# One kernel for two transformer blocks: rows remade in the first down projection, an absolute value in the bounded gates

## The chip, the cores and the metric

The kernel runs on one core of a Trainium2 chip. The core has TensorE (PE in the profile; PEld is its weight loads), VectorE (DVE), ScalarE (ACT), GpSimd (POOL) and SyncE (SP), which issues the DMAs. The metric is the device time of one execution in microseconds. TensorE's clock is granted at one of two levels, 2.4 GHz (1.00 in the profile) or 1.2 GHz (0.50).

## The reference

Everything is float32. A first block of two layers works on 256 latent tokens and 256 context tokens of width 1024; a second block of two layers works on the 256 latent tokens. The parts that the change touches:

```python
def _modulate(x, g, shift, scale):
    return _rmsnorm(x, g) * (1 + scale) + shift

def _swiglu(h, w1, w3, w2):                      # D_FF = 2816
    return (jax.nn.silu(h @ w1) * (h @ w3)) @ w2

def _forget(f_raw, lb):
    log_f = jnp.logaddexp(jnp.log(lb), jnp.log1p(-lb) + jax.nn.log_sigmoid(f_raw))
    k = (1.0 - lb) * jax.nn.sigmoid(-f_raw)
    return k, log_f

for l in range(DEPTH):                           # first block, DEPTH = 2
    lat = lat + 0.5 * ml[2] * _swiglu(_modulate(lat, norm_ffn1_g[l], ml[0], ml[1]), *ffn1)
    cx = cx + 0.5 * mc[2] * _swiglu(_modulate(cx, norm_ffn1_g[l], mc[0], mc[1]), *ffn1)
    # token mixer: gMLP and a bidirectional gated scan, whose gates come from _forget
    lat = lat + ml[5] * out_lat
    lat = lat + 0.5 * ml[8] * _swiglu(_modulate(lat, norm_ffn2_g[l], ml[6], ml[7]), *ffn2)
    if not last:
        cx = cx + mc[5] * out_cx
        cx = cx + 0.5 * mc[8] * _swiglu(_modulate(cx, norm_ffn2_g[l], mc[6], mc[7]), *ffn2)
```

The bounds `lb` are zero in layer 0, so only layer 1 has the logaddexp. It is computed as max(a, b) + ln(1 + exp(-|a - b|)).

## The kernel before

**Layout.** Tokens lie along the free dimension, channels on the 128 partitions: X is [128, 8 blocks, 512 tokens]. All weights stream from HBM in 272 slots of 1 MB, each 1024 x 256, in the order of the program. Every product is made in three matmuls (L583 to L585, helper `three`): each operand is split into a high part and the rest (WH and WL of the weights, HH and HL or GH and GL of the activations), and high times high, high times rest and rest times high are summed in PSUM. A slot with 256 tokens has 48 such matmuls, with kin = 6 it has 36.

**A slot's way.** SyncE loads RAW once the slot two before has been split. ScalarE copies it to WH in two halves (L1412) when TensorE has finished the slot two before (`mm_done`). VectorE subtracts for the first half of WL (L2016, one operation over 1024 elements), GpSimd for the second half (L1993, four operations over 256). TensorE waits for the first half at a slot's start and for the second at its fifth block (`slot_half`). Two pairs of PSUM banks alternate; a slot can start when the slot two before has been read out (`bank_read`).

**The plan.** `plan_slots` writes out the phases. A feed-forward part has three thirds of 8, 6 and 8 blocks; each third is an `ffn_up` phase (its slots hold w1 and w3 by turns) and a `down` phase of 4 slots. Each engine has its own program over this plan and runs it in order; in most phases it is a hardware loop of two slots (`repeat`), whose first instruction takes the waits ahead of it. After every slot each engine calls `after_slot`, which does its part of the split for the slot two later.

**Norms.** In four places a norm is made by stream (`norm_by_stream`): TensorE goes on with the context's tokens while the norm of the latents is still to come. The slots behind it begin in `pair_by_stream` (L803 on): blocks of 6 matmuls for stream 1, first of slot 0, from block 5 on by turns with slot 1, then `part_sums(3, 0)`, the last column sums of stream 0 (L665, a product of squares with ones), then five more blocks, and then stream 0, block by block behind `h_ready`. The sums go to VectorE's mean (L2150), ScalarE's root, VectorE's reciprocal (L2156) and then to T2 rows (L2162), HH (ScalarE L1468) and HL (L2168).

**The late norm.** The last feed-forward part of the first block (layer 1, 256 tokens) doesn't wait for its norm. Its rows are X times gain, without the norm's factor and without the shift; two more columns hold the shift, so that its matmuls have 258 columns. Behind each slot VectorE multiplies by RSTD (L2275, L2282) and adds the product of the shift (`shifted_up`, copies at L2273 and L2280, SHIFTED, L2287); ScalarE makes Silu (L1544) and GH (L1549), and VectorE then GL (L2033). All three thirds work so. In `down` VectorE adds bank times gate to X (L2444) behind each slot.

**The bounded gates.** In `w_in` of layer 1 the gates of two directions (d = 0, 1) are made behind slots 1 to 7 (`prepare`), in LF[d], KK[d] and T8, each [128, 2048]: VectorE adds a bound (L2749), takes a minimum (L2750), a maximum (L2754) and a difference (L2755); ScalarE makes Exp and Ln of T8 (L1867, L1868); VectorE adds it to LF (L2762). For d = 1 L2749 and L2750 are behind slot 5, L2754 and L2755 behind slot 6, the rest behind slot 7.

Of the kernel before, what the change touches and what calls it, by code (L numbers as in the profile page):

```python
# [28 lines left out]
KB = D // P  # L29
# [30 lines left out]
def plan_slots():  # L60
# [14 lines left out]
    def ffn(l, which, rate, tokens):  # L75
        if l + which == 2:
            plan.append(dict(kind="late_norm", gain="g_ffn2", layer=l, final=False, mods=(6, 7), ada=ada))
        else:
            do_norm(gain=("g_ffn1", "g_ffn2")[which], layer=l, mods=(0 + 6 * which, 1 + 6 * which), tokens=tokens,
                    first=(l == 0 and which == 0))  # L80
        for t, nb in enumerate(THIRDS):
# [4 lines left out]
            phase("ffn_up", nb, nb, rate, tokens=tokens, blocks=nb, layer=l, third=t, shifted=(l + which == 2))  # L86
# [6 lines left out]
            phase("down", 4, 4, rate, tokens=tokens, kin=nb, gate=2 + 6 * which, layer=l, per=1, first=(t == 0))  # L93
# [127 lines left out]
def build(nc, T):  # L221
    ctx = ExitStack()
    with ctx:
# [354 lines left out]
        def _(pe):  # L578
# [159 lines left out]
            def weights_phase(ph, normed, before):  # L738
                kind, N = ph["kind"], ph["tokens"] + (2 if ph.get("shifted") else 0)
                hbase = n.at(h_ready)  # L740
                loop = kind not in ("w_in", "in_even", "in_odd")

# [60 lines left out]
                def pair_by_stream():  # L803
# [21 lines left out]
                    for kb in range(KB):  # L825
                        if kb == ahead:
                            pe.wait_ge(bank_read[1], ph["unit"] + BANK_CREDIT)
                        if kb >= ahead:
                            block(1, 1, kb - ahead)
                        block(0, 1, kb)  # L830
                    part_sums(3, 0)
# [569 lines left out]
        def _(act):  # L1401
# [246 lines left out]
            def down(ph):  # L1648
# [3 lines left out]
                def body(it):  # L1652
                    for s in range(2 * ph["per"]):
                        after_slot(ph, it, s, 2 * ph["per"])
                        if ph["squares"] and s % ph["per"] == ph["per"] - 1:
# [11 lines left out]
                repeat(act, 2, body, ph is not PLAN[-1])  # L1667
# [182 lines left out]
            def prepare(ph, i):  # L1850
# [14 lines left out]
                if i in (3, 7) and l == 1:  # L1865
                    n.take(dve_to_act)
                    link(act.activation(T8[:], T8[:], ACT.Exp))  # L1867
# [138 lines left out]
        def _(dve):  # L2006
# [416 lines left out]

            def down(ph):
# [4 lines left out]
                def body(it):  # L2429
                    for v in range(2):  # L2430
                        for s in range(per):
                            after_slot(ph, it, per * v + s, 2 * per)
                        if v and ph["ends_by_stream"]:
                            add_unit(True, slice(0, N))
                        dve.wait_ge(mm_done, it * (2 * per) + (ph["slot"] + per * v + per))
# [12 lines left out]
                repeat(dve, 2, body, ph is not PLAN[-1])  # L2448
# [287 lines left out]
            def prepare(ph, i):  # L2736
# [8 lines left out]
                if i in (2, 5) and l == 1:  # L2745
# [4 lines left out]
                    link(dve.tensor_tensor(T8[:], lf, bc(LBT[:, 0, d, :], 4), ALU.min))  # L2750
                if i in (2, 6) and l == 1:
                    d = (2, 6).index(i)
                    lf = LF[d][:]
                    link(dve.tensor_tensor(lf, lf, bc(LBT[:, 0, d, :], 4), ALU.max))  # L2754
                    dve.tensor_tensor(T8[:], T8[:], lf, ALU.subtract).then_inc(dve_to_act, 1)  # L2755
# [296 lines left out]
```

## Time and profile before

| | |
|---|---|
| median of 3 runs | 2616.95 us (2616.52 to 2617.7) |
| profiled execution | 2619.17 us, its span 2617.4 us |
| granted clock of TensorE, mean | 0.995 |
| PE busy | 2569.0 us, 98% |
| DVE, ACT, POOL busy | 1222.5, 1105.2, 889.7 us (47%, 42%, 34%) |
| DMA | 376.90 MB, mean 144 GB/s |
| POOL WL L1993 | 889.5 us in 1088 operations |

PE's busy time comes from modelled ends of pipelined matmuls, so the distance from one start to the next tells more than it. The span is that of one execution with the profiler; 1.8 us lie around it. Idle time of an engine counts only if TensorE stands behind it.

### The profile page before, as it was taken

Reading aid. Unit: us, or ns where it says so; the run is one execution under the profiler, and the core shown is the slowest. Engines: PE = TensorE matmul, PEld = TensorE weight load, DVE = VectorE, ACT = ScalarE, POOL = GpSimd, SP = SyncE. Lnnn points to the kernel's source line nnn. Section 1 sums busy time; section 2 is a strip of 40 time slices with the busy share of each in tenths; the row PEclk is TensorE's granted clock in tenths of the full one; section 3 lists DMA queues with packets and bytes.
Section 4 is the critical chain, followed back from the end, with each engine's and each line's share of the span. In section 5 each row is a group of like instructions: output and inputs, shape, how many; then the busy total and the mean of one; then the engine's idle time right before and its main releaser. Section 6 shows DMA issues by size and latency. Waiting matters only on the chain.

```text
span 2617.4 us, 43989 instructions
## 1 busy us (share of the span) xinstructions
PE 2569.0 (98%) x17111; PEld 2290.2 (87%) x17111; DVE 1222.5 (47%) x1865; ACT 1105.2 (42%) x1538; POOL 889.7 (34%) x1092
## 2 busy tenths in 40 slices
PE   7999999999999999999999999999999999999999
PEld 5777779988897777797777798899999999999999
DVE  4222325227752232252232257675567566656754
ACT  4322333635444122244122247544674554446533
POOL 1222222320022222222222226315554455553554
PEclk9999999999999999999999999999999999999999
DMA  7443543330034334433444433234544444552454
GB/s 282 141 168 140 165 149 117 139 128 1 33 120 146 145 145 145 145 110 132 145 145 145 145 138 133 110 109 180 184 169 165 137 161 177 182 185 100 164 188 147
DMA packets 58528, 376.90 MB, mean 144 GB/s; under 512 B 6223, under 2 KB 12007, under 8 KB 14216
## 3 DMA queue, kind: packets, MB, share of 16 engines
q1 hardware_dynamic: 56988, 371.53, 39.2%
q10 hardware_dynamic: 1388, 3.16, 0.8%
q8 instruction: 118, 1.93, 0.3%
q14 instruction: 34, 0.28, 0.0%
HBM read 370.46 MB, written 3.16 MB: 143 GB/s over the span
## 4 chain that ended last, share of the span: by engine, by line
issue 58%; POOL 22%; PE 17%; DVE 1%; POOLq 1%; DMA 0%; ACT 0%; SPq 0%; DVEq 0%; ACTq 0%
POOL WL L1993 22%; PE PSA L583 5%; PE PSA L585 5%; PE PSA L584 5%; PE PSA L1342 0%; POOLq L405 0%; PE PSA L1240 0%; PE PSA L1267 0%; DMA X<-in_x 0%; DMA RAW<-in_weights 0%; PE PSA L665 0%; POOLq L1991 0%; ACT WH L1412 0%; PE PSA L1258 0%; PE PSA L1228 0%
## 5 line engine op out<-in xcount | busy, mean ns | idle before, releaser
L1993 POOL TENSOR_TENSOR WL<-RAW,WH 128x256 fp32r<-128x256 f32 x1088 | 889.5, 846 | 1715.3 <-ACT WH L1412 1715.3
L1412 ACT ACTIVATE WH<-RAW 128x1024 fp32r<-128x1024 f32 x544 | 545.8, 1050 | 936.6 <-PE PSA L585 918.0
L2016 DVE TENSOR_TENSOR WL<-RAW,WH 128x1024 fp32r<-128x1024 f32 x272 | 339.6, 1249 | 1077.5 <-ACT WH L1412 1077.2
L583 PE MATMUL PSA<-HH,WH 128*128 128x512 f32 (+2 forms) x1664 | 596.3, 358 | 9.4 <-DVE WL L2016 3.4
L584 PE MATMUL PSA<-HL,WH 128*128 128x512 f32 (+2 forms) x1664 | 588.6, 354 | 0.0
L585 PE MATMUL PSA<-HH,WL 128*128 128x512 f32 (+2 forms) x1664 | 588.0, 353 | 0.0
L583 PE MATMUL PSA<-GH,WH 128*128 128x256 f32 (+1 forms) x1664 | 527.0, 317 | 6.8 <-DVE GL L2033 5.7
L584 PE MATMUL PSA<-GL,WH 128*128 128x256 f32 (+1 forms) x1664 | 521.0, 313 | 0.0
L585 PE MATMUL PSA<-GH,WL 128*128 128x256 f32 (+1 forms) x1664 | 520.8, 313 | 0.0
L583 PEld LDWEIGHTS PSA<-HH,WH 128*128 128x128 f32 x1664 | 315.7, 190 | 69.0 <-issue 17.6
L585 PEld LDWEIGHTS PSA<-HH,WL 128*128 128x128 f32 x1664 | 315.8, 190 | 43.2
L584 PEld LDWEIGHTS PSA<-HL,WH 128*128 128x128 f32 x1664 | 315.9, 190 | 41.3
L583 PEld LDWEIGHTS PSA<-GH,WH 128*128 128x128 f32 x1664 | 318.0, 191 | 30.2 <-issue 5.4
L584 PEld LDWEIGHTS PSA<-GL,WH 128*128 128x128 f32 x1664 | 318.0, 191 | 18.6 <-issue 0.5
L585 PEld LDWEIGHTS PSA<-GH,WL 128*128 128x128 f32 x1664 | 317.9, 191 | 18.3
L583 PE MATMUL PSA<-H2H,WH 128*128 128x256 f32 x800 | 230.6, 288 | 0.5 <-DVE S L2346 0.5
L584 PE MATMUL PSA<-H2L,WH 128*128 128x256 f32 x800 | 226.3, 283 | 0.0
L585 PE MATMUL PSA<-H2H,WL 128*128 128x256 f32 x800 | 226.3, 283 | 0.0
L583 PEld LDWEIGHTS PSA<-H2H,WH 128*128 128x128 f32 x800 | 153.4, 192 | 2.3 <-issue 1.7
L584 PEld LDWEIGHTS PSA<-H2L,WH 128*128 128x128 f32 x800 | 153.5, 192 | 1.3 <-issue 1.0
L585 PEld LDWEIGHTS PSA<-H2H,WL 128*128 128x128 f32 x800 | 153.4, 192 | 0.0
L2033 DVE TENSOR_TENSOR GL<-T,GH 128x256 f32 (+3 forms) x168 | 136.0, 844 | 16.0 <-ACT GH L1568 10.6
(336 smaller groups left out, 2966.1 us busy)
## 6 DMA issues: line engine op xcount, KB each, us to landing
RAW<-in_weights SPq DMA_DIRECT2D x272, 1024.0 KB, 4.8
ADA<-in_w_ada SPq DMA_DIRECT2D x65, 1024.0 KB, 4.9
Zada<-in_w_ada SPq DMA_DIRECT2D x7, 1024.0 KB, 14.5
scratch_bias<-BREL ACTq DMA_DIRECT2D x1, 2048.0 KB
SUMS<-in_c_sums SPq DMA_DIRECT2D x1, 1664.0 KB, 8.7
TB<-scratch_bias SPq DMA_DIRECT2D x1, 1536.0 KB, 11.8
X<-in_x SPq DMA_DIRECT2D x1, 1024.0 KB, 6.8
X<-in_ctx SPq DMA_DIRECT2D x1, 1024.0 KB, 9.3
```

Of the source, the lines that this page charges most:

```text
L583: pe.matmul(out, a_hi, b_hi, start=start, stop=False)
L584: pe.matmul(out, a_hi, b_lo, start=False, stop=False)
L585: return pe.matmul(out, a_lo, b_hi, start=False, stop=stop)
L1412: act.activation(WH[:, j, 4 * h:4 * h + 4, :], RAW[:, j, 4 * h:4 * h + 4, :], ACT.Copy)\
L1993: ins = pool.tensor_tensor(WL[:, j, kb, :], RAW[:, j, kb, :], WH[:, j, kb, :].bitcast(F32), ALU.subtract)
L2016: dve.tensor_tensor(WL[:, j, 0:4, :], RAW[:, j, 0:4, :], WH[:, j, 0:4, :].bitcast(F32), ALU.subtract)\
L2033: return dve.tensor_tensor(out, value, hi.bitcast(F32), ALU.subtract)
```

## The change

Three edits. First, in the last feed-forward part of the first block only the first third still has the late norm. In its down projection each of the four slots makes two rows anew, now with RSTD and shift: VectorE T2 = X * scale * RSTD, ScalarE HH = T2 + shift, VectorE HL = T2 + shift - HH, between the split of weights and the addition to X (the rows of X that are read are the ones that are added to right behind it). The second and third third take these rows in 256 columns with the plain `ffn_up`. TensorE takes all eight `h_ready` before the second third's loop. Down's loop is written out on VectorE and ScalarE there. Second, `part_sums(3, 0)` stands in front of the last block of slot 0 instead of behind it. Third, in the bounded gates VectorE's minimum becomes a difference, the later difference goes, and ScalarE has an Abs in front of Exp, which takes a scale of -1.

```diff
--- before.py
+++ after.py
@@ -73,6 +73,7 @@
         plan.append(dict(kind="norm", index=norm, slot=slot, unit=unit, ada=ada, **more))
         norm += 1
     def ffn(l, which, rate, tokens):
+        at = len(plan)
         if l + which == 2:
             plan.append(dict(kind="late_norm", gain="g_ffn2", layer=l, final=False, mods=(6, 7), ada=ada))
         else:
@@ -83,14 +84,16 @@
                 plan.append(dict(kind="decays", part=2 * t - 1))
             if l + which == 0 and t:
                 plan.append(dict(kind=("", "setup_loads", "setup")[t]))
-            phase("ffn_up", nb, nb, rate, tokens=tokens, blocks=nb, layer=l, third=t, shifted=(l + which == 2))
+            phase("ffn_up", nb, nb, rate, tokens=tokens, blocks=nb, layer=l, third=t, shifted=(l + which == 2 and t == 0),
+                  renewed=(l + which == 2 and t == 1))
             if l + which == 0 and t == 2:
                 plan.append(dict(kind="bounds"))
             if t == 0:
                 plan.append(dict(kind="gate", layer=l, mod=2 + 6 * which, half=True, ada=ada))
             if l + which == 2:
                 plan.append(dict(kind="decays", part=2 * t))
-            phase("down", 4, 4, rate, tokens=tokens, kin=nb, gate=2 + 6 * which, layer=l, per=1, first=(t == 0))
+            phase("down", 4, 4, rate, tokens=tokens, kin=nb, gate=2 + 6 * which, layer=l, per=1, first=(t == 0),
+                  renews=plan[at] if l + which == 2 and t == 0 else None)
     for l in range(2):
         both, lat = 512, (512 if l == 0 else 256)
         ffn(l, 0, 1, both)
@@ -739,6 +742,8 @@
                 kind, N = ph["kind"], ph["tokens"] + (2 if ph.get("shifted") else 0)
                 hbase = n.at(h_ready)
                 loop = kind not in ("w_in", "in_even", "in_odd")
+                if ph.get("renewed"):
+                    n.take(h_ready, KB)
 
                 def h_block(kb):
                     pe.wait_ge(h_ready, hbase + kb + 1)
@@ -827,8 +832,9 @@
                             pe.wait_ge(bank_read[1], ph["unit"] + BANK_CREDIT)
                         if kb >= ahead:
                             block(1, 1, kb - ahead)
+                        if kb == KB - 1:
+                            part_sums(3, 0)
                         block(0, 1, kb)
-                    part_sums(3, 0)
                     for kb in range(KB - ahead, KB):
                         block(1, 1, kb)
                     for j in range(2):
@@ -1652,6 +1658,12 @@
                 def body(it):
                     for s in range(2 * ph["per"]):
                         after_slot(ph, it, s, 2 * ph["per"])
+                        if ph.get("renews"):
+                            for m in range(2):
+                                n.take(t_ready)
+                                kb = 4 * it + 2 * s + m
+                                act.activation(HH[:, kb, 0:N], T2[:, m, 0:N], ACT.Identity,
+                                               bias=MODS[:, ph["renews"]["mods"][0], kb, 0:1]).then_inc(hh_ready, 1)
                         if ph["squares"] and s % ph["per"] == ph["per"] - 1:
                             v = s // ph["per"]
                             act.wait_ge(bank_read[v], it * 2 + (ph["unit"] + 2 + BANK_CREDIT))
@@ -1664,7 +1676,7 @@
                                     .then_inc(sq_ready, 1)
                 if ph["ends_by_stream"]:
                     return body(0)
-                repeat(act, 2, body, ph is not PLAN[-1])
+                repeat(act, 2, body, ph is not PLAN[-1] and not ph.get("renews"))
                 if ph["squares"]:
                     n.squares += KB
 
@@ -1864,7 +1876,8 @@
                     act.activation(KK[:, d], KK[:, d], ACT.Exp).then_inc(act_to_dve, 1)
                 if i in (3, 7) and l == 1:
                     n.take(dve_to_act)
-                    link(act.activation(T8[:], T8[:], ACT.Exp))
+                    link(act.activation(T8[:], T8[:], ACT.Abs))
+                    link(act.activation(T8[:], T8[:], ACT.Exp, scale=-1.0))
                     act.activation(T8[:], T8[:], ACT.Ln, bias=1.0).then_inc(act_to_dve, 1)
                 if i == 8:
                     vs = VS[:, 0:4 * (N // P)]
@@ -2421,6 +2434,19 @@
                         after_slot(ph, it, per * v + per - 1, 2 * per)
                 n.skip(h_ready, KB)
 
+            def renewed_rows(late, k0, N):
+
+                shift, scale = late["mods"]
+                for m in range(2):
+                    if k0:
+                        dve.wait_ge(h_ready, n.at(h_ready) + k0 + m - 1)
+                    dve.scalar_tensor_tensor(T2[:, m, 0:N], X[:, k0 + m, 0:N], MODS[:, scale, k0 + m, 0:1], RSTD[:, 0:N],
+                                             ALU.mult, ALU.mult).then_inc(t_ready, 1)
+                for m in range(2):
+                    n.take(hh_ready)
+                    dve.scalar_tensor_tensor(HL[:, k0 + m, 0:N], T2[:, m, 0:N], MODS[:, shift, k0 + m, 0:1],
+                                             HH[:, k0 + m, 0:N].bitcast(F32), ALU.add, ALU.subtract).then_inc(h_ready, 1)
+
             def down(ph):
 
                 if ph["feeds"]:
@@ -2432,6 +2458,8 @@
                             after_slot(ph, it, per * v + s, 2 * per)
                         if v and ph["ends_by_stream"]:
                             add_unit(True, slice(0, N))
+                        if ph.get("renews"):
+                            renewed_rows(ph["renews"], 4 * it + 2 * v, N)
                         dve.wait_ge(mm_done, it * (2 * per) + (ph["slot"] + per * v + per))
                         for m in range(2):
                             for s, t in streams(N):
@@ -2445,7 +2473,9 @@
                             ins.then_inc(bank_read[v], 1)
                 if ph["ends_by_stream"]:
                     return body(0)
-                repeat(dve, 2, body, ph is not PLAN[-1])
+                repeat(dve, 2, body, ph is not PLAN[-1] and not ph.get("renews"))
+                if ph.get("renews"):
+                    n.skip(h_ready, KB)
                 if ph["rate"]:
                     rows_copy(ph)
 
@@ -2747,12 +2777,11 @@
                     lf = LF[d][:]
                     dve.wait_ge(lb_landed, 48)
                     link(dve.tensor_tensor(lf, lf, bc(LBT[:, 1, d, :], 4), ALU.add))
-                    link(dve.tensor_tensor(T8[:], lf, bc(LBT[:, 0, d, :], 4), ALU.min))
+                    link(dve.tensor_tensor(T8[:], lf, bc(LBT[:, 0, d, :], 4), ALU.subtract))
                 if i in (2, 6) and l == 1:
                     d = (2, 6).index(i)
                     lf = LF[d][:]
-                    link(dve.tensor_tensor(lf, lf, bc(LBT[:, 0, d, :], 4), ALU.max))
-                    dve.tensor_tensor(T8[:], T8[:], lf, ALU.subtract).then_inc(dve_to_act, 1)
+                    dve.tensor_tensor(lf, lf, bc(LBT[:, 0, d, :], 4), ALU.max).then_inc(dve_to_act, 1)
                 if i in (3, 7):
                     d = (3, 7).index(i)
                     n.take(act_to_dve)
```

VectorE in the first down projection, second pass of its two slots (T_62 is T2, the two rows and their rests); before:

```order
L2016 TENSOR_TENSOR WL<-RAW,WH 128x1024 [waits hi_ready]
L2444 ISA [waits mm_done]
L2444 ISA
L2444 SCALAR_TENSOR_TENSOR X<-PSA,MODS,X 128x256
L2444 ISA x2
L2444 SCALAR_TENSOR_TENSOR X<-PSA,MODS,X 128x256
```

and with the change:

```order
L2029 TENSOR_TENSOR WL<-RAW,WH 128x1024 [waits hi_ready]
L2443 SCALAR_TENSOR_TENSOR T_62<-X,MODS,RSTD 128x256 [waits h_ready] x2
L2447 SCALAR_TENSOR_TENSOR HL<-T_62,MODS,HH 128x256 [waits hh_ready] x2
L2472 SCALAR_TENSOR_TENSOR X<-PSA,MODS,X 128x256 [waits mm_done]
L2472 SCALAR_TENSOR_TENSOR X<-PSA,MODS,X 128x256
```

Four operations have come between the split and the two additions that free the bank.

TensorE where the first down projection ends and the second third's `ffn_up` begins; before:

```order
L585 MATMUL PSA<-GH,WL 128x256
L405 REGISTER_ALU
L405 COMPARE_AND_BRANCH
L405 UNCONDITIONAL_BRANCH
L405 ISA
L589 REGISTER_ALU [waits bank_read0]
L583 MATMUL PSA<-HH,WH 128x258 [waits lo_ready0]
```

and with the change:

```order
L588 MATMUL PSA<-GH,WL 128x256
L408 REGISTER_ALU
L408 COMPARE_AND_BRANCH
L408 UNCONDITIONAL_BRANCH [waits h_ready]
L408 ISA
L592 REGISTER_ALU [waits bank_read0]
L586 MATMUL PSA<-HH,WH 128x256 [waits lo_ready0]
```

The branch into the loop now has a wait for the rows, and the matmuls have two columns less.

VectorE in `w_in` of layer 1, behind slots 6 and 7 (T_102 is T8, LF_95 is LF[1]); before:

```order
L2754 TENSOR_TENSOR LF_95<-LF_95,LBT 128x2048
L2755 TENSOR_TENSOR T_102<-T_102,LF_95 128x2048 [waits dve_chain]
L2016 TENSOR_TENSOR WL<-RAW,WH 128x1024 [waits hi_ready]
L2760 TENSOR_TENSOR Ztm<-Ztm,LBK 128x2048 [waits act_to_dve]
L2762 TENSOR_TENSOR LF_95<-LF_95,T_102 128x2048 [waits act_to_dve,dve_chain]
```

and with the change:

```order
L2784 TENSOR_TENSOR LF_95<-LF_95,LBT 128x2048
L2029 TENSOR_TENSOR WL<-RAW,WH 128x1024 [waits hi_ready]
L2789 TENSOR_TENSOR Ztm<-Ztm,LBK 128x2048 [waits act_to_dve]
L2791 TENSOR_TENSOR LF_95<-LF_95,T_102 128x2048 [waits act_to_dve,dve_chain]
```

The difference is gone; the last addition still stands behind ScalarE.

## Rows read from the trace of the kernel before

**Rows 1.** The page: busy time, share and instructions of each engine.
```profile
PE 2569.0 (98%) x17111; PEld 2290.2 (87%) x17111; DVE 1222.5 (47%) x1865; ACT 1105.2 (42%) x1538; POOL 889.7 (34%) x1092
```

**Rows 2.** Waits of TensorE: waiter <- releaser: us in total, times, longest us.
```profile
PE PSA L583 <- DVE GL L2033: 5.7, 3, 2.9
...
PE PSA L583 <- POOL WL L1993: 4.0, 2, 2.8
```

**Rows 3.** Windows of TensorE: stretch, us, busy (matmuls), granted clock, DMA share, GB/s.
```profile
1628.80:1634.00 5.20, 5.19 (x24) 0.50 0.57 202
1870.70:1873.80 3.10, 3.10 (x15) 0.50 0.78 243
```

**Rows 4.** Timeline of TensorE, last norm by stream: start, us, operation [idle <-releaser].
```profile
1545.37 0.28 PE L585 MATMUL PSA<-WH,HL 128*128 128x256 f32 x1
1546.40 0.39 PE L583 MATMUL PSA<-WH,HH 128*128 128x256 f32 x1 [0.75 <-DVE HL L2168]
```

**Rows 5.** Timelines of ScalarE and VectorE in the same norm.
```profile
1537.34 0.71 ACT L1427 ACTIVATE S<-X 128x256 f32<-128x256 f32 x2
...
1542.10 0.42 DVE L2150 TENSOR_SCALAR RSTD<-PSA 128x256 f32<-128x256 f32 x1 [3.12 <-PE PSA L665]
```

**Rows 6.** Windows of TensorE, 258 columns and 256 columns, nothing but matmuls.
```profile
1890.00:1930.00 40.00, 40.00 (x335) 1.00 0.54 193
2440.00:2480.00 40.00, 40.00 (x336) 1.00 0.47 172
```

**Rows 7.** Timeline of TensorE in w_in of layer 1, slot 8.
```profile
1628.81 0.58 PE L583 MATMUL PSA<-HH,WH 128*128 128x256 f32 x1 [2.81 <-POOL WL L1993]
```

**Rows 8.** Timeline of GpSimd in w_in of layer 1.
```profile
1611.08 22.50 POOL L1993 TENSOR_TENSOR WL<-RAW,WH 128x256 fp32r<-128x256 f32 x12 [9.78 <-ACT WH L1412]
```

**Rows 9.** Timeline of VectorE in w_in of layer 1, behind slots 6 to 8.
```profile
1623.80 2.71 DVE L2755 TENSOR_TENSOR T<-T,LF 128x2048 f32<-128x2048 f32 x1
1626.43 1.75 DVE L2016 TENSOR_TENSOR WL<-RAW,WH 128x1024 fp32r<-128x1024 f32 x1
...
1634.04 2.29 DVE L2762 TENSOR_TENSOR LF<-LF,T 128x2048 f32<-128x2048 f32 x1 [3.14 <-ACT T L1868]
```

**Rows 10.** Timeline of ScalarE in w_in of layer 1, behind slot 7.
```profile
1624.95 2.00 ACT L1412 ACTIVATE WH<-RAW 128x1024 fp32r<-128x1024 f32 x2 [5.88 <-DMA RAW<-in_weights]
...
1628.81 1.91 ACT L1867 ACTIVATE T<-T 128x2048 f32<-128x2048 f32 x1
```

**Rows 11.** Groups by form: xcount | busy us, mean ns of one | idle before.
```profile
L2168 DVE SCALAR_TENSOR_TENSOR HL<-T,MODS,HH 128x256 fp32r<-128x256 f32 x64 | 32.9, 514 | 3.7 <-ACT HH L1468 3.7
L2487 DVE SCALAR_TENSOR_TENSOR X<-X,PR,RSTD 128x256 f32<-128x256 f32 x8 | 7.3, 957 | 0.0
```

**Rows 12.** Timelines at the end of the first down projection, one engine each.
```profile
1829.91 0.28 PE L583 MATMUL PSA<-HH,WH 128*128 128x258 f32 x1
1830.12 2.01 ACT L1412 ACTIVATE WH<-RAW 128x1024 fp32r<-128x1024 f32 x2 [3.66 <-PE PSA L585]
1831.21 1.23 DVE L2016 TENSOR_TENSOR WL<-RAW,WH 128x1024 fp32r<-128x1024 f32 x1 [3.66 <-ACT WH L1412]
1832.35 0.87 DVE L2444 SCALAR_TENSOR_TENSOR X<-PSA,MODS,X 128x256 f32 x2
1832.20 2.90 POOL L1993 TENSOR_TENSOR WL<-RAW,WH 128x256 fp32r<-128x256 f32 x4 [2.75 <-ACT WH L1412]
```

**Rows 13.** Timeline of TensorE in the second down projection.
```profile
1870.67 0.55 PE L583 MATMUL PSA<-GH,WH 128*128 128x256 f32 x1 [2.91 <-DVE GL L2033]
```

**Rows 14.** Timelines of VectorE and ScalarE at the second third's end.
```profile
1866.01 1.23 DVE L2016 TENSOR_TENSOR WL<-RAW,WH 128x1024 fp32r<-128x1024 f32 x1 [2.48 <-ACT WH L1412]
...
1867.88 1.78 DVE L2287 SCALAR_TENSOR_TENSOR T<-T,SHIFTED,S 128x256 f32<-128x256 f32 x2
1868.92 0.42 ACT L1549 ACTIVATE GH<-T 128x256 f32 x1 [2.00 <-DVE T L2287]
1869.58 1.28 DVE L2033 TENSOR_TENSOR GL<-T,GH 128x256 f32 x2
```

## The prediction

> **What bounds the kernel now.** I read the page first, then who TensorE waited for, then the timeline around each wait. TensorE is busy 98% of the span [rows 1], so no other engine's busy time is worth anything by itself; an edit counts only where it shortens TensorE's own row of matmuls or one of the few places where that row stops. Those are in the waits: three stops behind GL, one long one behind GpSimd's WL [rows 2], and at four places a stop of 0.75 us behind HL. All of the change's edits lie at such places, so the sum below is one of stops removed, moved and made. A hidden size matters throughout: after a stop of about 3 us the granted clock was 0.50, which is 1.2 instead of 2.4 GHz, for the next 3 to 6 us [rows 3].
>
> **Part 1, the column sums in front of the last block (norms by stream).** In a norm by stream TensorE does the column sums (L665), then 30 weight matmuls whose last starts at 1545.37, and the next one starts only at 1546.40, after 0.75 us of idle behind HL [rows 4]. The chain is sums, mean (L2150 at 1542.10, for which VectorE had stood idle 3.12 us behind L665), root, reciprocal, row, HL; the squares that L665 reads were made by ScalarE from 1537.34 to 1538.05 [rows 5]. So nothing but TensorE's order holds the chain. The change takes the sums 6 matmuls earlier. The pace of such matmuls is 40.00 us over 335, 0.120 us [rows 6], so the chain starts 0.72 us earlier, and the sums (0.22 us each, four of them, before 1542.10 less 0.72) still begin 2 us after the squares. The stop of 0.75 us falls to nearly nothing, and the eight rows behind it, which come one by one from VectorE, all come 0.72 us earlier. TensorE's own matmuls stay the same in number. The same stop stands in the trace at 442.99, 762.67 and 1154.54, so it is 4 x 0.72 = **-2.9**. Bounds: 0 (if a row behind the first is set by something else) and -3.0.
>
> **Part 2, the bounded gates (w_in of layer 1).** VectorE loses one operation over 2048 elements in each direction, ScalarE gets one. In the first direction nothing waits. In the second, TensorE stood 2.81 us until 1628.81 for GpSimd's WL [rows 7], because GpSimd's twelve operations took 22.50 us there against 2.90 for four elsewhere [rows 8, 12], with VectorE busy on long two-operand operations all the while. The removed one is L2755, 1623.80 to 1626.43 [rows 9]. Without it GpSimd's last three operations for that slot have VectorE out of the way from 1623.8 on and end near 1623.8 + 3 x 0.73 = 1626.0, about when TensorE comes to need them (24 matmuls after the slot's start at 1622.96, 1625.84). That removes 2.8 us or a little more, and also the low clock behind it: 24 matmuls in 5.2 us instead of 2.9, 2.3 us [rows 3]. So the slot would end 5.3 us earlier (3.0 of stop and 2.3 of clock). But it is given back two slots later. ScalarE's chain on T8 begins behind the weights of 1624.95 and an eviction, not behind L2755; the tile's pass costs 1.91 us [rows 10], so the added Abs moves the end of Ln from 1633.95 to 1635.85. On VectorE L2762 (2.29 us) and then the split for slot 10 stand behind it [rows 9]: 1635.9 + 2.3 = 1638.2, and with a GpSimd operation that gets in between (1.75 for the split, as in the row at 1626.43) 1640.0. TensorE came to this slot at 1641.3 before (1628.8 + 5.2, 1.5 of modulation matmuls, 48 x 0.12); now it is there at 1636.0 and waits 4.0 us. It starts 1.3 us earlier than before, and pays one low-clock stretch of its own (15 matmuls in 3.10 us instead of 1.8, 1.3 us [rows 3]). I take **0**. Bounds: -5.3 (nothing given back) and +1.5 (low clock as long as at 1628.8).
>
> **Part 3, rows remade in the first down projection.** Per slot VectorE gets two T2 rows and two HL rows between its weight split and the eviction of X, ScalarE two HH rows. No row of before shows this pair of operations there. The price of T2 (two SBUF operands, one of them RSTD) is in L2487, 0.957 us, and L2287 beside GpSimd took 1.78 for two [rows 14]; the lower bound is L2168, mean 0.514 [rows 11]. I take 0.95 for all four, less 0.07 of overlap between neighbours, since GpSimd starts its four operations 0.15 us before the first (1832.20 against 1832.35) [rows 12].
>
> By the Trainium skill (SBUF — State Buffer, Who interferes with whom) VectorE and GpSimd hold a shared port as an exclusive lock, so a two-operand row must wait for the GpSimd operation under way. The trace agrees in L2487 but not for most of L2168; by that rule HL costs 0.95, by the row 0.51, which would make the sum 1.8 us smaller.
>
> Slot end to slot end: ScalarE 1830.12, split 1831.21, free at 1832.35 [rows 12]. Then T2 until 1833.3 and 1834.2, HL until 1835.1 and 1836.0; HH, on ScalarE, lies beside them. Two effects on TensorE:
> (a) The eviction of the first slot now ends 3.6 us later, 6.7 us after the slot's end, and slot 3 needs that bank after 5.76 us (48 x 0.120). Stop of 1.25 us, once; the next one just fits. Bounds 0 and 2.5.
> (b) Between the last matmul on GL and the first on HH, which stand 0.12 us apart now (1829.91) [rows 12], TensorE must wait for all eight rows, since its branch into the loop waits for h_ready and not block by block. Rows 6 and 7 begin only after the slot's end, so it resumes near 1836.05: **+6.1**. Bounds 4.5 (0.48 each) and 7.5. With (a) **+7.35**. What covers all other rows is the down projection itself; only the last pair has no cover.
> (c) Behind this stop a low clock: **+1.3**, as after 1870.67 [rows 3, 13]. Bounds 0.3 and 2.7.
>
> **Part 4, what the two later thirds gain.** Before the second down projection TensorE stood 2.91 us for GL until 1870.67 [rows 13], in a low clock afterwards. Behind the split of 1866.01 stood a copy, two products and two L2287 (1867.88, 1.78 us), and only then GL at 1869.58 [rows 14]. Now the split, which ends at 1867.15 but for the overlap, is followed by a product with PSUM (0.44 us, half of L2444's 0.87 [rows 12]), GH (0.42) and GL at 1868.1: 1.5 us earlier, -1.5, and the stop that remains, 1.4 us, is as long as the other two behind GL (5.7 less 2.9, over 2 [rows 2]), behind which the clock stayed full: -1.4. Before the third one the stop of 1.4 us goes: -1.45. Together **-4.35**, bounds -2.9 and -4.6. The one in the first third stays.
>
> Two columns less in 14 x 48 = 672 matmuls: 335 of 258 columns ran in 40 us, and 336 of 256 [rows 6], so **0**, bounds 0 and -0.25. The Trainium skill (TensorE: Matmul & The Clock Gate, "Wait — 56ns, not 53.3ns?") has a matmul take its columns at 2.4 GHz plus a fixed part; by that rule this would be an estimate of -0.56 us. The trace says the columns don't set the pace here.
>
> **Sum:** -2.9 + 0 + 7.35 + 1.3 - 4.35 = **+1.4 us**. The profiled execution took 2619.17, which gives 2620.6; against the median of the runs, 2616.95, it is 2618.4. I predict 2618.4.
>
> **Rivals.**
> A. The gate's gain is kept (slot 10's weights are early enough, because L2762 and the split meet no GpSimd operation and the clock stays full): 1.4 - 5.3 = -3.9, 2613.1. For it: 5.3 us really go. Against it: the chain on T8 is counted row by row and its start is set by a DMA landing, not by VectorE. Chance 0.14.
> B. The remade rows cost what L2168's mean says and HL's pair fits into the slot: (a) 0, (b) 4.5: 1.4 - 2.85 = -1.45, 2615.5. For it: a mean of 0.514 over 64 says that hardly any waited. Against: L2487 and L2287. Chance 0.12. With A together it would be over 5.2 us faster.
> C. Slower: VectorE becomes the bound of the first down projection. It decides from 5.76 us of work per slot; mine is 1.14 + 3.6 + 0.8 = 5.5. If each of GpSimd's four operations (2.9 us in all) blocks VectorE once, it is 3.6 + 2.9 = 6.5; then the bank comes at 7.6, 14.1, and the last rows at 26.7 us instead of 24.6 from the first slot's end: +2.05. Longer stops also bring the longer low clock (1.3 more here, and 1.3 more in the gate): +6.1, 2623. Without the clock 2620.5. Chance 0.13.
> D. The rows are not late, the branch's wait being met early: (b) and (c) go, 1.4 - 7.4 = -6, 2611. Against: rows 6 and 7 stand behind the last slot's split in the program. Chance 0.03.
> My forecast has 0.58.
>
> **Numbers.** What a measurement can tell from no change is 0.2%, 5.2 us: 2611.7 to 2622.2. Nearly all cases lie inside. Faster needs D or A with B: 0.06. Slower needs C with its clock, or part 1 failing beside a low clock: 0.12. Same 0.82. The range that holds 8 in 10 goes from 2613.1 (A) to 2622.4 (short of C with its clock); the likeliest case's own is 2615.5 to 2621.5.
>
> **What would show it.** Right: the stop behind HL in the norms by stream nearly gone (four times); no stop of 2.8 us in w_in's slot 8 but one near 4 us before slot 10; a stop near 6 us before the second third's first matmul, with a low clock behind it, and one of about 1.2 us in the first down projection; the stop before the second down projection halved, the third's gone; T2 rows at 0.95 us. Wrong: T2 and HL at 0.48, a stop before the second third under 4.5 us, or w_in shorter by over 2 us. The whole is wrong if the time leaves 2613 to 2622.

## The result and the profile after

| | before | after |
|---|---|---|
| median of 9 runs each | 2617.36 us (2614.96 to 2618.88) | 2622.27 us (2619.63 to 2625.3) |
| profiled execution's span | 2617.4 us | 2620.5 us |
| ratio to before | | 1.0019, 95% interval 1.0011 to 1.0028 |

The change costs 4.9 us by the medians (2.9 to 7.3 by the interval) and 3.1 us between the two profiles. The time, 2622.27, lies 0.13 us inside the stated range; the size, +1.4, was too small. Two executions of this study, one of before (11561.66 us) and one of the kernel of experiment 8 (4878.45 us), lie far off all others and count in no ratio. First the waits of TensorE after, against [rows 2] (columns as there):

```profile
PE PSA L586 <- DVE HL L2447: 6.1, 1, 6.1
...
PE PSA L586 <- ACT Zfm L1704: 4.0, 1, 4.0
...
PE PSA L586 <- DVE GL L2046: 2.5, 2, 1.4
PE PSA L586 <- DVE X L2472: 2.3, 2, 1.2
...
PE PSA L586 <- DVE HL L2181: 1.1, 4, 0.3
```

Each forecast stop is there: 6.1 us for the rows, 4.0 in the gates, two stops behind GL in place of three, and the norms by stream with 0.3 where 0.75 stood. Of the two behind X the first, in the first down projection, was forecast; the second was not.

Matching TensorE's 17111 matmuls of the two traces one by one, I get after less before at each place (below, the ledger). It starts at -0.5 (before any edit acts) and goes to -3.4 behind the four norms (**-2.9**, forecast -2.9); to -8.6 at the end of w_in's slot 8, -9.1 ahead of slot 10, and back to -3.4 behind slot 10 (**0.0**, forecast 0); +1.3 (bank), +6.35 (rows) and +2.1 (low clock) to +6.5 (**+9.75**, forecast 8.65); -1.8 and -1.3 at the second down projection, +0.9 ahead of the third third, -1.55 at the third (**-3.75**, forecast -4.35). The rest, to +3.1, is 0.15 of low clock in the mixer and 0.4 at 2164, where TensorE waits 0.9 us for VectorE's S in place of 0.5.

Behind the last slot of the first down projection, VectorE, GpSimd and TensorE (the answer to [rows 12], start, us, operation, [idle <-releaser]):

```profile
1829.35 1.23 DVE L2029 TENSOR_TENSOR WL<-RAW,WH 128x1024 fp32r<-128x1024 f32 x1 [0.22 <-ACT WH L1418]
1830.49 1.81 DVE L2443 SCALAR_TENSOR_TENSOR T<-X,MODS,RSTD 128x256 f32<-128x256 f32 x2
1832.22 1.80 DVE L2447 SCALAR_TENSOR_TENSOR HL<-T,MODS,HH 128x256 fp32r<-128x256 f32 x2
1833.95 0.86 DVE L2472 SCALAR_TENSOR_TENSOR X<-PSA,MODS,X 128x256 f32<-128x256 f32 x2
```
```profile
1830.34 3.41 POOL L2006 TENSOR_TENSOR WL<-RAW,WH 128x256 fp32r<-128x256 f32 x4 [2.28 <-ACT WH L1418]
```
```profile
1827.94 0.28 PE L588 MATMUL PSA<-GH,WL 128*128 128x256 f32 x1
1834.36 0.58 PE L586 MATMUL PSA<-HH,WH 128*128 128x256 f32 x1 [6.13 <-DVE HL L2447]
```

and the window of TensorE right behind the stop (columns as in [rows 3]):

```profile
1834.36:1839.00 4.64, 4.64 (x22) 0.50 0.63 226
```

A remade row costs 0.9 us twice (1.81 and 1.80 for two), as taken from L2487 in [rows 11]; GpSimd's four operations beside them took 3.41 against 2.90. In w_in the chain on ScalarE is the one worked out, with Abs in front (the answer to [rows 10]), and behind it the eviction that TensorE is said to wait for:

```profile
1623.94 1.92 ACT L1879 ACTIVATE T<-T 128x2048 f32<-128x2048 f32 x1
1625.87 1.28 ACT L1880 ACT_TABLE_LOAD   x1
1627.16 1.92 ACT L1880 ACTIVATE T<-T 128x2048 f32<-128x2048 f32 x1
1629.10 1.28 ACT L1881 ACT_TABLE_LOAD   x1
1630.39 1.92 ACT L1881 ACTIVATE T<-T 128x2048 f32<-128x2048 f32 x1
1632.21 1.98 ACT L1418 ACTIVATE WH<-RAW 128x1024 fp32r<-128x1024 f32 x2
1634.21 1.28 ACT L1704 ACT_TABLE_LOAD   x1
1635.51 0.66 ACT L1704 ACTIVATE Zfm<-PSA 128x256 f32<-128x256 f32 x2
```
```profile
1632.41 2.29 DVE L2791 TENSOR_TENSOR LF<-LF,T 128x2048 f32<-128x2048 f32 x1 [5.85 <-ACT T L1881]
1634.74 1.62 DVE L2029 TENSOR_TENSOR WL<-RAW,WH 128x1024 fp32r<-128x1024 f32 x1
```

TensorE resumed at 1636.47; the eviction ended at 1636.17, and the first half of WL for the same slot at 1636.36, so two chains end there within 0.2 us. The prediction had counted only the second of them.

The stop that was not forecast, at the end of the second down projection: TensorE, then what stands behind it on VectorE, ScalarE and GpSimd.

```profile
1891.28 0.38 PE L586 MATMUL PSA<-HH,WH 128*128 128x256 f32 x1 [1.12 <-DVE X L2472]
```
```profile
1889.13 1.22 DVE L2029 TENSOR_TENSOR WL<-RAW,WH 128x1024 fp32r<-128x1024 f32 x1 [4.30 <-ACT WH L1418]
1890.28 0.87 DVE L2472 SCALAR_TENSOR_TENSOR X<-PSA,MODS,X 128x256 f32 x2
```
```profile
1877.17 2.01 ACT L1418 ACTIVATE WH<-RAW 128x1024 fp32r<-128x1024 f32 x2 [2.37 <-PE PSA L588]
...
1888.04 2.01 ACT L1418 ACTIVATE WH<-RAW 128x1024 fp32r<-128x1024 f32 x2 [4.30 <-DMA RAW<-in_weights]
```
```profile
1879.25 3.69 POOL L2006 TENSOR_TENSOR WL<-RAW,WH 128x256 fp32r<-128x256 f32 x4 [2.65 <-ACT WH L1418]
```

GpSimd ends the split at 1882.94, the load into the same half of RAW lands 5.1 us later, ScalarE copies, VectorE splits and only then adds to X, which frees the bank. From copy to copy that is 10.9 us (1877.17 to 1888.04) for two slots of 36 matmuls, 8.6 us of TensorE. In the kernel before, the stop at this place was 0.3 us. That the longer stop at 1867.5 had given the loop a lead there is a reading that no run tests by itself, but two profiles fit it: in experiments 2 and 7 (the kernel without remade rows), where the low clock behind that longer stop lasted 28 and 27 matmuls instead of 14, even that stop of 0.3 us is gone.

### The profile page after: what moved, and what is told of

Read it like the earlier page. It is cut to its first block, busy times and chain, and to the rows that moved or that the text cites. A ratio compares the mean times of both kernels' runs of the same rounds, so it can differ in the third digit from the quotient of the medians.

```text
span 2620.5 us, 43900 instructions
## 1 busy us (share of the span) xinstructions
PE 2568.7 (98%) x17111; PEld 2290.1 (87%) x17111; DVE 1214.8 (46%) x1837; ACT 1110.2 (42%) x1548; POOL 886.9 (34%) x1092
## 4 chain that ended last, share of the span: by engine, by line
issue 58%; POOL 22%; PE 17%; DVE 1%; POOLq 1%; DMA 0%; ACT 0%; SPq 0%; DVEq 0%; ACTq 0%
POOL WL L2006 22%; PE PSA L586 5%; PE PSA L588 5%; PE PSA L587 5%; PE PSA L1348 0%; POOLq L408 0%; PE PSA L1246 0%; PE PSA L1273 0%; DMA X<-in_x 0%; DMA RAW<-in_weights 0%; PE PSA L668 0%; POOLq L2004 0%; ACT WH L1418 0%; PE PSA L1264 0%; PE PSA L1234 0%
```

## The experiments

All were timed against the kernel before on the same chip, but on three chips in all (experiments 1 to 4; 5 to 7; 8 and 9), and after itself on its own occasion, so a difference between two rows of the table is surer by the ratios than by the medians. "Ledger" is the difference of matched matmuls between two traces.

| kernel | median, us | before, us | ratio (95%) |
|---|---|---|---|
| sums alone | 2614.41 | 2617.59 | 0.9989 (0.9980 to 0.9998) |
| gates alone | 2620.59 | 2617.59 | 1.0011 (1.0002 to 1.0020) |
| rows alone | 2625.23 | 2617.59 | 1.0025 (1.0013 to 1.0036) |
| after, Exp and Ln later | 2624.20 | 2617.59 | 1.0023 (1.0014 to 1.0032) |
| after, rows by block | 2614.77 | 2617.83 | 0.9987 (0.9978 to 0.9997) |
| after, factor and T2 in PSUM | 2619.83 | 2617.83 | 1.0006 (0.9996 to 1.0015) |
| after, these three | 2614.24 | 2617.83 | 0.9985 (0.9976 to 0.9994) |
| sums, gates, Exp and Ln later | 2617.02 | 2617.83 | 0.9997 (0.9988 to 1.0006) |
| after, V first | 2622.54 | 2618.80 | 1.0017 (1.0009 to 1.0026) |
| after, V first, by block, PSUM | 2612.34 | 2618.80 | 0.9979 (0.9970 to 0.9988) |
| sums, gates, V first | 2615.29 | 2618.80 | 0.9992 (0.9983 to 1.0001) |

**1. The sums alone.** Before, with the second edit of the diff:

```diff
+                        if kb == KB - 1:
+                            part_sums(3, 0)
                         block(0, 1, kb)
-                    part_sums(3, 0)
```

> The kernel before with the column sums moved in front of the last block, nothing else. My theory (the chain behind the sums is held only by TensorE's order): the four stops of 0.75 us behind HL are gone, -2.9 us, ratio 0.9989. Rival (later rows are set by something else): under 1 us. The spread of the runs stays as before, since no long stop is added.

-3.2 us by the medians (-0.5 to -5.2 by the interval); the ledger up to w_in has -2.9 (-0.4 to -3.3). The theory holds. Its profile showed something else: the stops of 2.8 and 2.9 us are still there, but the clock behind them stayed full. Windows of TensorE right behind those two stops, columns as in [rows 3], where the same places had 24 and 15 matmuls at 0.50:

```profile
1625.49:1630.69 5.20, 5.20 (x49) 1.00 0.58 205
1864.86:1867.96 3.10, 3.10 (x26) 1.00 0.71 240
```

**2. The gates alone.** Before, with the third edit:

```diff
-link(act.activation(T8[:], T8[:], ACT.Exp))
+link(act.activation(T8[:], T8[:], ACT.Abs))
+link(act.activation(T8[:], T8[:], ACT.Exp, scale=-1.0))
```

> The kernel before with the bounded gates alone changed (Abs on ScalarE, one VectorE operation less). My theory: the stop of 2.8 us and its low clock go (-5.6 us), and a stop of 4.0 us with a low clock of 1.5 us comes two slots later; net 0.0 us in a profile, 0 to +2 in the median, as the low clock behind a stop of 4 us may be longer in other runs. Rival A (gain kept): -5.3 us.

+3.0 us (+0.5 to +5.2): above the 0 to +2 that I had worked out, and not rival A. The stops are as said:

```profile
PE PSA L583 <- ACT Zfm L1692: 3.9, 1, 3.9
```

and the ledger against before, counted from w_in on, is -0.1 behind slot 10, as worked out. The rest comes later, in low clock at places where both kernels stop alike: +1.8 at the mixer's start in layer 1 (columns as in [rows 3], this kernel, then before),

```profile
1671.30:1676.00 4.70, 4.70 (x27) 0.60 0.00 0
```
```profile
1671.30:1676.00 4.70, 3.16 (x29) 0.98 0.00 0
1676.00:1682.60 6.60, 6.60 (x28) 0.50 0.00 0
```

(the clock of before fell there too, but 3.0 us behind the second stop, here 1.0) and +1.3 at the second down projection, where it lasted 28 matmuls here and 14 there. These differ between two executions, so one profile can't settle what the edit does on average. What it can say: the profile of before held 2.65 us of low clock behind the gate's stop, that of experiment 1 none.

**3. The rows alone.** Before, with the first edit, in TensorE's part:

```diff
+                if ph.get("renewed"):
+                    n.take(h_ready, KB)
```

> The kernel before with the rows remade in the first down projection alone. By the stops of the changed kernel's profile: +1.3 (bank) +6.4 (wait for eight rows) +2.1 (low clock) -3.1 (second down projection) +0.85 (a stop before the third third) -1.55 (third down projection) = +6.0 us. If the wider spread of the changed kernel's runs comes from the clock behind the 6.4 us stop, this kernel's runs spread over 4 us or more and its median lies above +6; if it comes from the gates, its runs lie within 2 us.

+7.6 us, runs 2622.48 to 2625.53, a spread of 3.1 us: above +6 as said, but narrower than 4. The three medians sum to +7.4 against +4.9 for all, within their intervals; which stop makes the after kernel's spread (5.7 us) these runs don't settle.

**4. Exp and Ln later.** After, with

```diff
+                if i in (3, 8) and l == 1:
                     link(act.activation(T8[:], T8[:], ACT.Exp, scale=-1.0))
```

and VectorE's addition to LF behind slot 8 as well.

> The changed kernel, with ScalarE's Exp and Ln of T8 for the second direction and VectorE's addition to LF moved behind slot 8 (Abs stays behind slot 7). My theory: ScalarE's row of three passes is what gave the gate's gain back; now the weights' high part for slot 10 and the eviction of slot 8 come before Exp and Ln, the stop of 4.0 us and its low clock go: -5.6 us against the changed kernel, about -0.7 us to -2 us against the one before by medians. Rival (the next chain on ScalarE and VectorE, the mean square of V, gets late instead): stop moved to a later slot, gain under 2 us.

2624.20, no gain against after (ratio 1.0023 and 1.0019): the rival was right. The stop before slot 10 is gone, and one as long stands before the spatial gate, which needs V:

```profile
1643.93 1.88 PE L964 MATMUL PSA<-WS,Ztm 128*128 128x128 f32 x12 [4.10 <-DVE Ztm L2806]
```

**5. Rows by block.** After, with

```diff
-                    n.take(h_ready, KB)
+                    n.skip(h_ready, KB)
...
+                elif ph.get("renewed"):
+                    body(0, first=True)
+                    repeat(pe, ph["slots"] // 2, body, loop, first=1)
```

and `h_block` before each block of its first slot.

> The changed kernel, with TensorE waiting for the remade rows block by block in the second third's first slot (its first two slots written out ahead of the loop) in place of one wait for all eight. My theory: the six rows that are there cover the last two; the stop of 6.3 us falls to about 1.2 us (the bank of the slot before, evicted behind the rows) and its low clock of 2.1 us goes: -7 us against the changed kernel, -2 to -3 us against the one before by medians, and the spread of the runs narrows. Rival (weights are loaded too late in the second third once the stop that let them catch up is gone): 2 us or more of stops come back in the second down projection, gain 4 us.

2614.77, 7.5 us less than after's 2622.27 (8 by the two ratios), and 3.1 us faster than before. TensorE at that place and the window behind it:

```profile
1829.51 0.39 PE L586 MATMUL PSA<-HH,WH 128*128 128x256 f32 x1 [0.96 <-DVE X L2475]
```
```profile
1829.51:1835.00 5.49, 5.49 (x45) 1.00 0.53 191
```

A stop of 1.0 us in place of 6.1, and the clock full. Ledger against after at this place: -7.2, of which 5.15 is the stop and 2.05 the clock. A stop of 0.5 us before the second third's third slot gives some of it back, and the two profiles end 7.1 us apart. Since only the way of waiting was changed (with two slots written out ahead of the loop for it), this shows that the wait for all eight rows was the cost.

**6. Factor and T2 in PSUM.** After, with

```diff
+                factor, T2 = bank(6)[:, 0:N], PSA[:, 5:8:2, :]
+                if k0 == 0:
+                    link(dve.tensor_scalar(factor, RSTD[:, 0:N], 1.0, None, ALU.mult))
```

> The changed kernel, with the factor RSTD copied into a PSUM bank and T2 of the remade rows in PSUM banks, so that no row operation has two SBUF tensors as inputs. If the rows cost 0.92 us because both inputs lie in SBUF beside GpSimd: T2 and HL fall to 0.45 to 0.5 us, GpSimd's four operations from 3.47 to 2.9 us, the bank stop of 1.3 us goes, the wait for the rows falls from 6.3 to 4.7 us: -3.0 us, up to -5 with a shorter low clock. Rival (these operations are simply slow at this size): the rows stay at 0.9 us and nothing changes.

2619.83, 2.4 us less than after (3.4 by the two ratios). VectorE and GpSimd behind the last slot:

```profile
1832.64 0.88 DVE L2446 SCALAR_TENSOR_TENSOR PSA<-X,MODS,PSA 128x256 f32<-128x256 f32 x2
1833.66 0.88 DVE L2450 SCALAR_TENSOR_TENSOR HL<-PSA,MODS,HH 128x256 fp32r<-128x256 f32 x2
```
```profile
1832.49 2.87 POOL L2006 TENSOR_TENSOR WL<-RAW,WH 128x256 fp32r<-128x256 f32 x4 [2.82 <-ACT WH L1418]
```

With one SBUF tensor as input a row costs 0.44 instead of 0.90, and GpSimd's four 2.87 instead of 3.41: neither engine holds up the other. The bank stop is gone, and the wait for the rows fell by 1.65 us (4.77 against 6.41 from start to start). The rival falls. The trace of before holds the other half of the proof: its rows L2168 have two SBUF inputs too (T2 and HH). Here is that line's record, and below it that of L2447 after (durations of one, ns: least, median, most):

```profile
L2168 DVE SCALAR_TENSOR_TENSOR HL<-T,MODS,HH x64: 477/480/927, 425.5 to 1552.0; 128x256 fp32r<-128x256 f32 x64
```
```profile
L2447 DVE SCALAR_TENSOR_TENSOR HL<-T,MODS,HH x8: 940/956/962, 1813.6 to 1833.1; 128x256 fp32r<-128x256 f32 x8
```

Set beside GpSimd's timeline, 40 of the 64 overlap none of its operations, and all 40 took 0.48. Of the other 24, four took 0.92, four 0.57, and sixteen, which began in the last 0.2 us of a GpSimd operation, 0.48. So two SBUF inputs alone are not slow; the neighbour makes them so.

**7. These three edits (4, 5 and 6) at once, and the same without remade rows** (before, with experiments 1, 2 and 4):

> The changed kernel with three edits at once: rows taken block by block, factor and T2 in PSUM, ScalarE's Exp and Ln spread behind slot 8. My theory: no stop over 1 us in the first down projection or before the second third, none before slot 10 of w_in: -15 us against the changed kernel, -10 to -12 against the one before, 2605 to 2607 us. Rival (load loop gives back 2 us or more in the second down projection): 2608.

> The kernel before with the column sums moved, the gates changed and ScalarE's Exp and Ln spread behind slot 8, but the late norm left as it was. Sum of the parts: -2.9 - 5.6 = -8.5 us, 2608.9 us. If the rows remade cheaply are worth anything, the kernel with all edits is faster than this one by 2 to 3 us.

2614.24 and 2617.02: 8 us short each. Both counted 5.6 us for the gates with Exp and Ln later; against the sums alone (ratio 0.9989) they cost some 2 us instead (0.9997). The rows, made cheaply, are worth 2.8 us between the two, though the two intervals overlap. A stop of 0.7 us came back before the third slot of the second third, behind ScalarE, which had the table loads for the decays ahead of its work.

**8. V first.** After, with V's mean square and root ahead of Exp (behind slot 9) and Ln (behind slot 10), in three combinations; ScalarE's part, and VectorE's for V's squares:

```diff
+                if i in (3, 9) and l == 1:
                     link(act.activation(T8[:], T8[:], ACT.Exp, scale=-1.0))
+                if i in (3, 10) and l == 1:
                     act.activation(T8[:], T8[:], ACT.Ln, bias=1.0).then_inc(act_to_dve, 1)
...
+                    sq = T8 if l == 0 else V[:, 2:4, :]
```

> The changed kernel, with VectorE's and ScalarE's work on V (mean square, root) left behind slot 8 but ahead of the rest of the gates: Exp of T8 for the second direction comes behind slot 9, Ln and the addition to LF behind slot 10, and V's squares go to a free half of V in place of T8. My theory: spreading Exp and Ln alone failed because V's chain stood behind them on both engines (stop of 4.4 us before the spatial gate); with V ahead, neither slot 10 nor the spatial gate waits: the 4.0 us stop and its low clock of 1.5 us go, -5.6 us against the changed kernel. Rival: Exp and Ln make the copies for slots 12 and 13 late, and 2 to 4 us come back there.

> The changed kernel with rows taken block by block, factor and T2 in PSUM, and V ahead of Exp and Ln: 2614.2 us (the kernel with the first two edits and Exp and Ln spread behind slot 8) less the 5.5 us that its stop before the spatial gate and the clock behind it cost: 2608.7 us, within 2 us. Rival (the gate's gain is given back once more): 2613 to 2614.

> The kernel before with the column sums moved, the gates changed and V ahead of Exp and Ln; the late norm is left as it was: -2.9 - 5.6 = -8.5 us, 2609.1 us. If the rows, remade cheaply and taken block by block, are worth something in themselves, the kernel with all edits is faster than this one; by the profiles (4.35 gained in the later thirds, 1.0 and 1.3 us of stops behind late weights given back) by 2 us.

2622.54 against 2622.27: nothing gained. Neither slot 10, nor the copies for slots 12 and 13, nor the spatial gate waited. The ledger against after runs to -5.6 and back to -0.9 at the mixer's start, through a longer stop and, more, a longer low clock behind it:

```profile
1662.60 0.79 PE L980 MATMUL PSA<-GHI,MEND 128*128 128x512 f32 x1 [3.68 <-DVE GLO L2048]
```

where 1.4 us stood before. TensorE from that stop on, this kernel, then after:

```profile
1662.60:1678.80 16.20, 15.65 (x62) 0.50 0.00 0
```
```profile
1666.02:1682.40 16.38, 14.84 (x85) 0.79 0.00 0
```

Of the 4.8 us given back here, 1.5 are stops and 3.3 the clock. I named two places for the stop to come back and it took a third. With the other edits this is the fastest kernel of the study, 2612.34, 0.9979 of before; its advantage over the same without rows (2615.29) is again 3 us, but it missed the 2608.7 that was forecast; the rival's 2613 to 2614 is nearer. Without rows the ratio is 0.9992, against 0.9989 for the sums alone: in no arrangement did the gates' edit gain anything that these runs can tell. The remaining combination (rows by block and in PSUM, the sums moved, the gates as before) was not run.

**9. Decay rows moved** behind the second down projection:

```diff
-            if l + which == 2:
+            if l + which == 2 and t != 1:
                 plan.append(dict(kind="decays", part=2 * t))
...
+                if t == 2:
+                    plan.append(dict(kind="decays", part=2))
                 plan.append(dict(kind="decays", part=2 * t - 1))
```

> The changed kernel with VectorE's two decay rows (DK) moved from the second down projection to behind it, nothing left out. The stop of 1.3 us before the third third stands behind VectorE's X, which stands behind a split whose weights landed late; the load of that slot was issued when GpSimd had done 3.69 us instead of 2.9 beside the decay rows. If the loop of load, copy and split is what holds it, the stop falls by 0.5 to 0.8 us. Rival (the loop is too long even so): it stays within 0.2 us.

One profiled run, 2628.12. The distance from start to start at that place fell from 1.40 to 0.66 us (TensorE):

```profile
1893.66 0.38 PE L588 MATMUL PSA<-HH,WH 128*128 128x256 f32 x1 [0.38 <-DVE X L2474]
```

so 0.74 us of it came through GpSimd's split, as the loop theory has it. But both parts of the decays now stand in a row; ScalarE waited 3.64 us for VectorE behind them, and TensorE stopped 3.35 us two slots later. Of the 5.85 us between this profile and after's, 3.3 lie ahead of the edit, in the first 610 us and mostly in their clock (below).

## Why the prediction held, and where its size was off

The stops and the sign held; that the time lies in the range was luck. 2622.27 is 0.13 us below the upper bound, and four of the nine runs lie above it. It is outside the likeliest case's own range (up to 2621.5) and 0.27 above the 2622 that was named as a sign of being wrong. From +1.4 to the ledger's +3.1, the terms are: +1.1 in part 3, +0.6 in part 4, +0.55 at two places that the sum had left out, and -0.5 from before any edit.

- **Part 1** was right in mechanism and size: -2.9 in the ledger, -3.2 by experiment 1.
- **Part 2**'s stops were right (2.8 away, 4.0 in return, TensorE back at 1636.47 where 1640.0 less 3.4 was forecast). The failed step is "and also the low clock behind it ... 2.3 us". I took the low clock of one profile as a fixed price of the stop. Over the profiles in which that stop is unchanged it was 2.65, 0 and 1.5 us (before, experiments 1 and 3), 1.4 on average. The gain of removing it is smaller on average, and the loss by the new, longer stop is not: low clock followed it in every profile that had it (1.5 to 2.2 us). That explains some 1.3 of the 3 us that the gates cost by the medians while the two profiles show 0; where the rest comes from isn't shown. The same holds for the -1.4 in part 4: 1.45, 0, 2.75, 2.6 and 1.3 us there (before, experiments 1 and 2, and the kernels without remade rows in 7 and 8).
- **Part 3** held: (a) 1.3 for 1.25, (b) 6.35 for 6.1, rows at 0.9 for 0.95. The reading "not for most of L2168" was mistaken: the mean of 0.514 mixes 40 rows that met no GpSimd operation with 24 that did (experiment 6), so it was no evidence for cheap rows and no lower bound beside GpSimd. (c) was sized by the stop of 3 us, 1.3; behind 6 us it was 2.1. Experiments 5 and 6 show (b) and the row's price as causes.
- **Part 4** gave 3.75 of 4.35. The step "the stop that remains" was right at both places; what was left out is the loop of load, copy and split, which gave 0.9 us back before the third third.
- **From profile to median.** Before's profiled execution was 1.8 us above the median of nine runs, after's at its median. A sum against one profile inherits its luck with the clock.
- **Rivals.** A fell (experiments 2, 4, 8): the gain from the removed operation never stayed. B fell, since the rows were blocked. C (2623) was nearer in time than the forecast (2618.4), but not in mechanism: VectorE did not become the bound, with 5.5 us of work in slots of 5.76. D fell: TensorE did stop 6.1 us for the rows.

How much the clock can shift a profile is seen where no edit acts. At the first layer's mixer TensorE has no wait over 0.15 us; it makes 32 matmuls of 2 columns one behind the other, and then the clock falls, for a time that differs from one execution to the next, and in one not at all. TensorE from 600 to 640 us in before, experiment 6 and the kernel without rows of experiment 8:

```profile
600.00:640.00 40.00, 38.65 (x291) 0.96 0.00 1
```
```profile
600.00:640.00 40.00, 38.65 (x275) 0.91 0.00 1
```
```profile
600.00:640.00 40.00, 37.98 (x298) 1.00 0.00 1
```

In the ledger that is +1.6 and -1.6 us against before. Four of the fourteen profiles have the +1.6, one the -1.6.

## What to carry to other kernels

When a later loop takes rows that the last slot makes, let the consumer wait block by block: six finished blocks covered two late ones, and a wait of 6.1 us shrank to 1.0. A stop removed ahead of a serial chain on ScalarE and VectorE can move to the chain's next consumer, as it did in experiments 4 and 8; sum that chain to the end of the phase before counting the gain. Price the low clock behind a stop of about 3 us as a chance (here 0 to 2.75 us), not as a sum read in one profile.

## What the runs showed of the hardware

- The same stop of 2.8 to 2.9 us is followed by full clock or by up to 28 matmuls at the lower level (0.50), from one execution to the next, with nothing changed at that place. Behind a stop of 1.4 us by itself it stayed full in all profiles of this study, behind one of 3.6 us and more inside the program it fell each time; behind the one of 3.35 us (experiment 9) it stayed full. At the mixer's start in layer 1, behind two stops of 1.4 and 1.5 us close together and matmuls of 2 columns, it fell in every profile with these two stops, but not at the same time: 1.0 us behind the second in experiment 2, 3.0 us in before. In layer 0 the same matmuls of 2 columns stand there without a stop, and behind them it fell in 13 of 14 profiles.
- VectorE's operation over 256 elements with two SBUF inputs lasts 0.96 us beside GpSimd's 256-element operations (one every 0.90), 0.48 with one input in PSUM (one every 0.44), and 0.48 with two SBUF inputs while no operation of GpSimd runs; GpSimd's pays too (0.85 against 0.72). By the Trainium skill (SBUF — State Buffer, Who interferes with whom) the two engines share a port under an exclusive lock; experiment 6 agrees, and its price here is a factor of two for VectorE.
